# Seven block products in place of eight in 20 of the 22 gated rounds of a feed-forward stage

## The reference

```
h = _rmsnorm(x, lw["norm_ffn_w"]) * (1 + sc_f) + sh_f
ffn = (jax.nn.silu(h @ lw["ffn_w1"]) * (h @ lw["ffn_w3"])) @ lw["ffn_w2"]
x = x + g_f * ffn
y = _rmsnorm(x, norm_final_w)
```

## Time and profile before

| | |
|---|---|
| median of three runs | 3107.42 us |
| span of the profiled execution | 3106.5 us |
| TensorE matmul busy | 3060.1 us, 99% of the span |
| VectorE, ScalarE, GpSimd busy | 50%, 39%, 24% |
| granted TensorE clock, mean | 0.997 of full speed |
| DMA | 250.61 MB, mean 81 GB/s |

### The profile page before, as it was taken

One profiled execution on the slowest core, in us unless ns is written; L12 is line 12 of the kernel. 1 busy time (PEld: TensorE's weight loads), 2 busy tenths in 40 slices (PEclk: granted clock), 3 DMA queues, 4 the chain that ended last, 5 costly groups with the idle time before them and its releaser, 6 DMA issues. The chain is left out here.

```text
span 3106.5 us, 59758 instructions
## 1 busy us (share of the span) xinstructions
PE 3060.1 (99%) x22180; PEld 2941.0 (95%) x22180; DVE 1539.3 (50%) x2647; ACT 1217.6 (39%) x2315; POOL 752.6 (24%) x936
## 2 busy tenths in 40 slices
PE   6999999999999999999999999999999999999998
PEld 5899999999999999999999999999999999999998
DVE  4646657568466574674656333444343222222233
ACT  6445455564554555545545442112241101210222
POOL 0024345245353462353534500000200000000002
PEclk9999999999999999999999999999999999999999
DMA  7622122122231221222212244434111111111112
GB/s 264 246 82 90 41 80 81 48 77 80 65 97 40 82 78 48 86 72 68 86 48 76 91 151 142 136 97 135 39 41 41 41 47 41 47 35 47 41 34 88
DMA packets 291362, 250.61 MB, mean 81 GB/s; under 512 B 10952, under 2 KB 262960, under 8 KB 291120
## 3 DMA queue, kind: packets, MB, share of 16 engines
q1 hardware_dynamic: 255552, 193.40, 20.3%
q10 hardware_dynamic: 35568, 54.02, 5.4%
HBM read 210.90 MB, written 36.47 MB: 80 GB/s over the span
## 5 line engine op out<-in xcount | busy, mean ns | idle before, releaser
L823 PE MATMUL bank<-h_hi,w_hi 128*128 128x384 f32 x2496 | 868.5, 348 | 2.5 <-ACT th L1416 2.5
L823 PE MATMUL bank<-h_hi,w_lo 128*128 128x384 f32 x2496 | 836.6, 335 | 0.0
L823 PE MATMUL bank<-h_lo,w_hi 128*128 128x384 f32 x2496 | 835.8, 335 | 0.0
L2147 PE MATMUL bank<-a_hi,v_hi 128*128 128x384 f32 x1440 | 483.1, 336 | 7.0 <-DVE v_lo L2367 2.5
L823 PEld LDWEIGHTS bank<-h_hi,w_hi 128*128 128x128 f32 x2496 | 469.4, 188 | 17.6 <-issue 7.3
L2147 PE MATMUL bank<-a_hi,v_lo 128*128 128x384 f32 x1440 | 481.1, 334 | 0.0
L2147 PE MATMUL bank<-a_lo,v_hi 128*128 128x384 f32 x1440 | 481.1, 334 | 0.0
L823 PEld LDWEIGHTS bank<-h_lo,w_hi 128*128 128x128 f32 x2496 | 469.8, 188 | 2.7
L823 PEld LDWEIGHTS bank<-h_hi,w_lo 128*128 128x128 f32 x2496 | 469.0, 188 | 0.0
L1935 POOL TENSOR_TENSOR kq<-kq,fg 128x384 f32<-128x384 f32 x288 | 290.0, 1036 | 176.3 <-PE bank L952 145.0
L2147 PE MATMUL bank<-b_hi,v_hi 128*128 128x384 f32 x912 | 306.3, 336 | 0.9 <-DVE v_lo L2367 0.9
(11 more groups left out here) (278 smaller groups left out, 4376.5 us busy)
## 6 DMA issues: line engine op xcount, KB each, us to landing
raw<-in_w_in SPq DMA_DIRECT2D x104, 512.0 KB, 4.1
cumb<-cum_scratch SPq DMA_DIRECT2D x72, 512.0 KB, 6.0
raw<-in_ffn_w SPq DMA_DIRECT2D x60, 512.0 KB, 3.8
ada_late<-in_ada_w SPq DMA_DIRECT2D x8, 2048.0 KB, 9.4
small<-gate_scratch ACTq DMA_DIRECT2D x72, 192.0 KB, 2.4
gate_scratch<-th ACTq DMA_DIRECT2D x48, 192.0 KB, 1.9
y_scratch<-x_t SPq DMA_DIRECT2D x8, 1152.0 KB, 4.8
small<-y_scratch ACTq DMA_DIRECT2D x48, 192.0 KB, 2.4
```

The costliest lines, as they stand in the source:

```text
L823: last = pe.matmul(out, w[i][:, k, :], h[:, k, blk(hb)], start=(k == 0 and j == 0), stop=(k == KT - 1 and j == 2))
L2147: last = pe.matmul(banks[3 * s + b][:, 0:BW], wp[s][:, k, :], operand[ap][:, k, blk(b)], start=(k == 0 and j == 0), stop=(k == kt - 1 and ...
```

## The change

It does three things.

First, of the 22 gated rounds two stay as they are (`PLAIN`), and 20 use a block scheme with seven products in place of eight. The operands of a round are divided in two each way: the weights by halves of the contraction (4 of 8 tiles, `KH`) and by `ffn_w1` against `ffn_w3`, the activations by halves of the contraction and of the tokens (576 columns, `HALF`). A product is done for two quarters of the tokens (`SUB` = 288 columns) of 4 x 3 matmuls each, so a round has 7 x 2 x 12 matmuls. Three of the seven weight blocks are parts of the loaded tiles; four are sums of such parts (S1 to S4), made by GpSimd (`s_sums_of`) for every round. The activation sums (T1 to T3 and a fourth, which is written over a quarter of `a_hi`, `a_lo`) are made once, mostly by VectorE, beside the two plain rounds. The seven weight blocks are cast by ScalarE (`x_high_part`) and split by VectorE (`x_low_part`) into seven slots, one for each product (`ring`), while the round before runs. Products 4, 5 and 6 add to a bank that an earlier product has filled; `keep_p1`, `add_u2`, `add_c22`, `add_c12` and `add_c21` combine the results on the vector side, `tanh1`, `tanh2`, `gate1`, `gate2` and `hid_product` make the hidden tile.

Second, the hidden tile of 128 x 1152 is stored to memory (`store_hid`, 576 KB) each round and is read back in pieces of 128 x 384 (`load_hid`, three buffers), cast and split.

Third, the down projection comes once at the end, token third by token third: 24 units of 22 x 3 matmuls of 384 columns. `ffn_w2` is loaded, cast and split once for each third, in five blocks (`K_BLOCKS`) with a slot each. Of the three pieces of a unit's weights (`load_down`) each uses `raw[n % 2]`. Rows of a finished third are turned back, scaled and stored beside the units of the next.

Semaphores used in the setup are cleared by GpSimd at the beginning of this stage and used again. SBUF places are laid over old ones.

```diff
+SUMS = {1: 2, 2: 1, 3: 3, 5: 4}
+PLAIN = 2
+ROUNDS = HID - PLAIN
+BLOCKS = 7
+STEPS = 2 * BLOCKS
+T2, T1, T3 = 0, 1, 2
+K_BLOCKS = (0, 4, 8, 12, 16, HID)
+QS = len(K_BLOCKS) - 1
+OUTS = KT
...
+    def ring(o):
+        if o < 3:
+            return xh_hi[:, o], xh_lo[:, o]
+        ks = slice(KH * ((o - 3) % 2), KH * ((o - 3) % 2) + KH)
+        return w_hi[(o - 3) // 2][:, ks, :], w_lo[(o - 3) // 2][:, ks, :]
+
+    def ring_source(o):
+        if o in SUMS:
+            return s_sums[(SUMS[o] + 1) % 2][:, :].rearrange("p (k c) -> p k c", c=P)
+        return {0: raw[0][:, 0:KH, :], 4: raw[0][:, KH:KT, :], 6: raw[1][:, KH:KT, :]}[o]
...
+    def bank_of(o, j):
+        return banks[{0: 0, 1: 2, 2: 4, 3: 6, 4: 0, 5: 4, 6: 6}[o] + j]
...
+            def load_pair(rd):
+                for s in range(2):
+                    sp.dma_start(raw[s][:, :, :], w_src((m["ffn_w1"], m["ffn_w3"])[s][0], rd * P + PLAIN * P)
+                                 ).then_inc(x_raw[s], 16)
+
+            def store_hid(rd):
+                sp.wait_ge(hid_done, rd * 4 + 4)
+                dst = hid_dram[rd + PLAIN] if isinstance(rd, int) else hid_dram[bass.ds(rd + PLAIN, 1)].rearrange(
+                    "a p n -> p (a n)")
+                sp.dma_start(dst, small_all[:, T:2 * T]).then_inc(hid_stored, 16)
...
+            with sp.Fori(0, ROUNDS - 1) as rd:
+                sp.wait_ge(x_split, rd * BLOCKS + BLOCKS)
+                load_pair(rd + 1)
+                store_hid(rd)
+
+            def load_down(u, c):
+
+                n, t = 3 * u + c, u % OUTS
+                if n < 2:
+                    sp.wait_ge(x_split, ROUNDS * BLOCKS)
+                else:
+                    pu, pc = divmod(n - 2, 3)
+                    sp.wait_ge(x_split, ROUNDS * BLOCKS + QS * pu + (2, 4, 5)[pc])
+                kt = min(8, HID - 8 * c)
+                sp.dma_start(raw[n % 2][:, 0:kt, :],
+                             w_src(m["ffn_w2"][0, 8 * c * P:(8 * c + kt) * P, :], t * P)).then_inc(x_raw[n % 2], 16)
...
+            load_down(0, 0)
+            load_down(0, 1)
+            store_hid(ROUNDS - 1)
+            load_down(0, 2)
...
+            def pair(rd, first=False):
+
+                for o in range(BLOCKS):
+                    pe.wait_ge(x_split, rd * BLOCKS + (o + 1))
+                    w = ring(o)
+                    if first and o in (1, 2, 3, 6):
+                        pe.wait_ge(t_split, {1: 1, 2: 2, 3: 3, 6: 4}[o])
+                    for j in range(2):
+                        if first and o == 0:
+                            pe.wait_ge(freed, free_at("up0", PLAIN - 1, 0, j))
+                        elif first and o == 1 and j == 0:
+                            pe.wait_ge(freed, free_at("up0", PLAIN - 1, 1, 2))
+                        elif o == 0:
+                            pe.wait_ge(gate1_done, rd * 2 + (j - 1))
+                        elif o == 1 and not first:
+                            pe.wait_ge(u2_done, rd * 2 + (j - 1))
+                        elif o == 2 and not first:
+                            pe.wait_ge(c12_done, rd * 2 + (j - 1))
+                        elif o == 3 and not first:
+                            pe.wait_ge(c21_done, rd * 2 + (j + 1))
+                        elif o == 4:
+                            pe.wait_ge(p1_kept, rd * 2 + (j + 1))
+                        elif o in (5, 6):
+                            pe.wait_ge(c22_done, rd * 2 + (j + 1))
+                        out = bank_of(o, j)[:, 0:SUB]
+                        for k, (hi, lo) in enumerate(moving(o, j)):
+                            for i, (wi, mv) in enumerate(((0, hi), (0, lo), (1, hi))):
+                                last = pe.matmul(out, w[wi][:, k, :], mv, start=(o < 4 and k == 0 and i == 0),
+                                                 stop=(k == KH - 1 and i == 2),
+                                                 skip_group_check=o >= 4)
+                        last.then_inc(prod_done, 1)
+
+            def down(u):
+
+                b, t = divmod(u, OUTS)
+                if u >= 2:
+                    pe.wait_ge(d_added, u - 1)
+                else:
+                    pe.wait_ge(gate1_done, 2 * (ROUNDS - 1) + u + 1)
+                out = banks[u % 2][:, 0:BW]
+                for q in range(QS):
+                    pe.wait_ge(x_split, ROUNDS * BLOCKS + QS * u + q + 1)
+                    w = d_ring(q)
+                    for k in range(K_BLOCKS[q], K_BLOCKS[q + 1]):
+                        if t == 0:
+                            pe.wait_ge(hid_split, HID * b + k + 1)
+                        for i, (wi, mv) in enumerate(((0, hid_hi[b]), (0, hid_lo[b]), (1, hid_hi[b]))):
+                            last = pe.matmul(out, w[wi][:, k - K_BLOCKS[q], :], mv[:, k, :],
+                                             start=(k == 0 and i == 0), stop=(k == HID - 1 and i == 2))
+                    last.then_inc(d_multiplied, 1)
...
+            def x_high_part(rd, o, first=False):
+
+                at_source(act, rd, o)
+                if first:
+                    act.wait_ge(unit_done, done("o", 3, 1, 2) if o < 3 else done("up0", PLAIN - 1, (o - 3) // 2, 2))
+                else:
+                    act.wait_ge(prod_done, rd * STEPS + (2 * o + 2 - STEPS))
+                act.activation(ring(o)[0], ring_source(o), ACT.Copy).then_inc(x_high, 1)
...
+            def pair(rd):
+                for j in range(2):
+                    keep_p1(rd, j, isinstance(rd, int) and rd == 0)
+                for o in range(4):
+                    x_high_part(rd + 1, o)
+                for j in range(2):
+                    tanh1(rd, j)
+                x_high_part(rd + 1, 4)
+                tanh2(rd, 0)
+                x_high_part(rd + 1, 5)
+                tanh2(rd, 1)
+                x_high_part(rd + 1, 6)
+
+            def load_hid(h):
+
+                b, k = divmod(h, HID)
+                if h >= NB * HID:
+                    return
+                if k < PLAIN:
+                    act.wait_ge(first_stored, 16 * PLAIN * NB)
+                else:
+                    act.wait_ge(hid_stored, 16 * (k + 2 - PLAIN))
+                if h < 3:
+                    act.wait_ge(x_split, ROUNDS * BLOCKS)
+                else:
+                    act.wait_ge(hid_split, h - 2)
+                act.dma_start(hid_in[h % 3], hid_dram[k, :, blk(b)]).then_inc(hid_landed[h % 3], 16)
+
+            def hid_high_part(h):
+
+                b, k = divmod(h, HID)
+                act.wait_ge(hid_landed[h % 3], 16 * (h // 3 + 1))
+                if b == 0:
+                    act.wait_ge(prod_done, (ROUNDS - 1) * STEPS + (4 if k < 6 else 6 if k < 12 else 8))
+                elif b == 1:
+                    act.wait_ge(prod_done, ROUNDS * STEPS)
+                else:
+                    act.wait_ge(d_multiplied, QS * OUTS)
+                act.activation(hid_hi[b][:, k, :], hid_in[h % 3], ACT.Copy).then_inc(hid_high, 1)
+                load_hid(h + 2)
...
+            def last_pair(rd):
+                for j in range(2):
+                    keep_p1(rd, j)
+                load_hid(0)
+                load_hid(1)
+                for h in range(8):
+                    hid_high_part(h)
+                tanh1(rd, 0)
+                d_high_part(0, 0)
...
+            def t_fourth():
+
+                ch = t_step
+                second = slice(HALF, T)
+                dve.wait_ge(unit_done, plain_done)
+                dve.wait_ge(t_split, 1)
+                to = a_sum[:, 0:KH, second]
+                ch.add(dve.tensor_tensor(to, a_hi[:, KH:KT, 0:HALF].bitcast(F32), t_hi[:, T2].bitcast(F32),
+                                         ALU.subtract))
+                ch.wait(dve)
+                ch.add(dve.tensor_tensor(to, to, t_lo[:, T2].bitcast(F32), ALU.subtract))
+                ch.wait(dve)
+                dve.tensor_tensor(to, to, a_lo[:, KH:KT, 0:HALF].bitcast(F32), ALU.add).then_inc(t_summed, 1)
...
+            def add_c22(rd, j):
+                dve.wait_ge(prod_done, rd * STEPS + (6 + j + 1))
+                dve.wait_ge(u2_done, rd * 2 + (j + 1))
+                dve.wait_ge(hid_stored, rd * 16 + 16)
+                dve.tensor_tensor(kept_v[:, 2 + j], kept_u[:, j], bank_of(3, j)[:, 0:SUB], ALU.add).then_inc(u3_done, 1)
+                dve.wait_ge(u3_done, rd * 2 + (j + 1))
+                dve.tensor_tensor(kept_v[:, 2 + j], kept_v[:, 2 + j], bank_of(2, j)[:, 0:SUB],
+                                  ALU.add).then_inc(c22_done, 1)
+
+            def gate1(rd, j):
+                dve.wait_ge(tanh_done, rd * 4 + (j + 1))
+                dve.scalar_tensor_tensor(kept_g[:, j], kept_th[:, j], 1.0, bank_of(4, j)[:, 0:SUB], ALU.add,
+                                         ALU.mult).then_inc(gate1_done, 1)
+
...
+            def gate2(rd, j):
+                dve.wait_ge(tanh_done, rd * 4 + (j + 3))
+                dve.wait_ge(c12_done, rd * 2 + (j + 1))
```

(157 more changed lines are left out.)

561 lines of the change are left out of this document (372 added, 189 removed).

## The result

The changed kernel takes 3121.11 us (median of 4 runs, 3119.73 to 3122.63) against 3108.06 for the kernel before beside it: ratio 1.0041, 95% interval 1.0027 to 1.0055. It is 0.4% slower; 3102 was forecast. The profiled execution spans 3117.9 us where before spanned 3106.5: 11.4 to explain.

The account below looks back on a forecast made before the run. TensorE was taken to bound the kernel before, the helper loop the new rounds. Rounds -24.7, plain rounds +1.2, first down unit +14.9, clock +4, end -0.9 made -5.5: 3102 us, range 3083 to 3138.

Parts of the forecast that it names:

- Price of 288 columns: TensorE: a 288-column matmul in the new rounds costs 0.1333 us, streaming plus a fixed 0.0133.
- rival C: Gated rounds: narrower matmuls get no cheaper than 0.173 us, round 29.1, time about 3206; chance 0.03.
- Ceiling of a round 22.4: TensorE's own work in a gated round: 168 matmuls, 22.4 us, 2.6 less than before.
- Turn 23.1: Helper loop from SP store to store: sets each of 18 gated rounds at 23.1 us, through add_c22.
- Plain rounds +1.2: Two plain rounds at the entry: start 1.2 us late because low(2) stands behind two sums.
- Clock +4: Both ends: long TensorE waits lower the granted clock, charged half of some 4 us at each, +4.
- First round 34.1: First seven-product round: 34.1 us, product 5 starting at about 27.7 instead of 16.0 because the next pair loads late.
- First down unit +14.9: Exit: the first down unit ends 14.9 us late, behind hidden tiles read back and the last weight chunk.
- End -0.9: Near the kernel's end: the old wait on v_lo goes, with its restart, -0.9 us.
- -5.5: Whole kernel: the net change forecast in the profiled span, us, giving 3101.0 from 3106.5.
- B: SP's store ahead of the loads: transfers stretch the loop, slower; turn 24.4 gives 3125, upper bound 3154; chance 0.32.
- A: Gated rounds: TensorE sets them, loop turn 22.4 or less, 3089, or 3084 with a cheaper exit; chance 0.25.

Follow-up runs that it names:

- e1: Changed kernel with SP issuing the next two weight loads ahead of the store of the round just ended: 3092.83 us, ratio to before 0.9955.
- e2: Changed kernel with GpSimd's fourth weight sum made over only 4 of its 128 columns a tile: 3114.19 us, ratio to before 1.0021.
- e3: Changed kernel with the subtractions making v_lo at the entry moved ahead in VectorE's order, the first before all operand sums: 3118.22 us, ratio to before 1.0034.
- e5: Changed kernel with GpSimd's one wide operand sum at the entry made by VectorE instead: 3116.52 us, ratio to before 1.0027.
- e4: Changed kernel with the third chunk of the first down unit's weights loaded ahead of the last hidden store: 3117.69 us, ratio to before 1.0035.
- e7: e4 plus last gated tile's first third cast from SBUF, norm weights loaded later, second down unit's loads held for the last gated tile: 3116.64 us, ratio 1.0029.
- e6: e1 with the first gated round's own small VectorE and ScalarE work ahead of the next round's weight splits: 3091.29 us, ratio to before 0.9944.
- e9: e1 with pair 0's last two splits ahead of the fourth operand sum, so pair 1 loads earlier: 3082.29 us, ratio to before 0.9913.
- e10: e9 plus e7's exit with second down unit's loads held one tile less, and a reordered entry with all wide sums on VectorE: 3074.37 us, ratio 0.9883.

## Why the prediction missed

The mechanism was as told: matmuls cheaper, the round set by the helper loop through `add_c22`, both ends paid for. Three terms of the sum were too small, the turn of the loop, the plain rounds and the clock, and together they turned the sign.

- **Price of 288 columns**, 0.1333: measured 0.1325. Right, so rival C falls. Ceiling of a round 22.4: measured 22.26 in e1.
- **"Turn 23.1", the first step that failed.** From the second round to the last, `keep_p1` starts at 2359.14 and 2785.58, 18 rounds: 23.69 apart on average (the first 22.3, then 23.5 to 23.9): +10.6 us over 18. Link by link in the turn shown above, forecast then measured: store and loads 6.5, 7.19; S1, S2 3.1, 2.81; cast and split 1.5, 1.27; `c22` and third split 1.6, 1.54; S3 and cast 2.2, 2.18; fourth split to `c12` 2.6, 2.72; `tanh2`, `gate2` 1.2, 0.97; the second of these 1.6, 1.89; products and SP 2.6, 3.21. That is 23.78 against 22.9. The transfers are 0.7 over. Operations that VectorE and GpSimd held up for each other are 0.34 + 0.55 (the two splits) + 0.46 (the product at 2643.29) = 1.35 us of the turn, most of the excess in the products among them; the other links together were 1.2 under the forecast. I had priced two engines at work together from a row where GpSimd took 1.20 for 1.02, a small loss; e2, e3 and e5 show that an operation can lose nearly the whole overlap. Of the 1.35 only the 0.34 was taken away by an experiment (e2); the rest is read from the trace.
- **"Plain rounds +1.2", the second.** Measured +9.0: a wait of 6.5, and 2.5 for matmuls at a clock of 0.50 behind it, which stand 0.32 apart in place of 0.173. I counted two sums of 2.55 ahead of `low(2)`. Even at that length they leave a wait of 3.6 (e5), because TensorE needs `v_lo` at 2287.5 and the sums start at 2284.9; 2.9 more came from the first sum, which took 5.50 while GpSimd's sum ran. In e3 and e5 a part of what was won here came back as waits in pair 0.
- **"Clock +4", the third.** What the three places lost beyond their waits is 2.5 in the plain rounds, 2.9 in the first gated round and 5.8 in the first down unit, some 11 us (an estimate, from the distances of the starts). It is counted in the other items.
- **First round 34.1**: measured 35.8; the wait was 10.2 where I had 11.7, and the clock made it longer.
- **First down unit +14.9**: measured +15.2, but that the numbers agree is luck. The waits are 9.4 (8.0 for `hid_lo`, where I had about 14) and the clock of 0.50 is the rest; and the tile loads took up to 7.3 us behind weight traffic (e4, e7), which I had not in the sum.
- **End -0.9**: measured -0.8.
- Added up, measured less forecast: gated rounds +11.7 (the turn 10.6, first and last round 1.1), the old rounds 0.4 shorter than 499.6, plain rounds +7.8, first down unit +0.3, end +0.1, upstream +0.5, and -4 for the clock, which is inside the others: +16.9 before rounding, which with -5.5 makes +11.4.

Of the rivals, B named the place, SP's store ahead of the loads, and e1 shows it: that order alone is worth 27 us by the ratios. Its size, 23.7 to 23.8, was between my 23.1 and B's 24.4. A was wrong of this kernel; what it says, that TensorE sets the rounds, is true of e1.

The Trainium skill (SBUF — State Buffer, section SBUF: two separate sides) says that VectorE, with two inputs in SBUF, and GpSimd share a port pair as an exclusive lock, which the first to start holds for its whole instruction. The traces agree: 2.96 lost of 3.1 in common, and GpSimd loses in its turn when it comes second (an S2 of 3.50 us at 2306.60, 1.30 else, behind a wide split of VectorE that ended at 2308.9; the product of 1.27 us at 2643.29). By that rule the first sum would have been 5.5 and the plain rounds near +4 even before the clock; I had not drawn on it.

Left open: the 0.5 us upstream of the changed rounds; why store and loads take 7.2 and not 6.5 (0.92 of it is SP's step from store to load; the loads alone take 5.7 to 5.8 in e1, where I had 5.4); and how much of the exit is the three landing buffers, since a fourth was not tried.

## What to carry to other kernels

In a loop over several queues, add up the turn, and look first at what stands ahead of the load that starts the next turn: here one store, ahead of two loads, cost 27 us, half of the 54 us that 20 rounds of 22.26 in place of 24.96 could give, and decided between slower and faster. Where VectorE and GpSimd both work on SBUF inputs, VectorE on two, price the overlap as one behind the other, not side by side. And removing a wait at the start of a loop only moved it here (e6), until the load that was late was issued earlier (e9).

## What the runs showed of the hardware

- An operation of VectorE with two SBUF inputs, started while one of GpSimd ran, lost all but some 0.14 us of the time in common: 5.50 for 2.55 (3.09 in common), 4.18 for 1.22 (3.08), 1.03 for 0.69 (0.48); with one input in PSUM it lost nothing (0.55 as alone). An operation of GpSimd that started second lost likewise: 3.50 for 1.30, 1.27 for 0.81.
- The starts of matmuls at full clock were 132.5 ns apart with 288 columns and 173.3 with 384, which is N / 2.4 ns + 12.5 and 13.3 ns.
- Two loads of 512 KB behind a store of 576 KB: the first sum started 7.19 us after the store's issue, with 0.92 us between the issues of store and first load; with the loads ahead of the store it started 5.68 to 5.83 us after the first load's issue.
- Waits of about 1.3 us in each 23.7 left the clock at 1.00; it was 0.50 behind waits of 10.2 and 6.5 us, and fell to it during one of 5.2. Behind a wait of 2.5 us in e10 it was 0.50 too, for a shorter time (from 2334 to 2336, 0.66 over 4 us). In the first down unit it stayed at 0.50 from 2818 to 2834, while TensorE worked in pieces between waits.
